# A float32 transformer layer on one core: first feed-forward block in two phases, modulation sums spread over later stages

## The chip, the core and the metric

The kernel runs on one core of a Trainium2 chip. The metric is the device time in microseconds of that core, from start to end of one execution. The median of three runs of the kernel before is 2205.12 us (2204.97 to 2205.4).

## What is computed

One layer over 1024 latent tokens `x` and 256 context tokens `ctx`, width 1024, all in float32: a SwiGLU feed-forward block of hidden width 2816, a mixer (retention heads and chunked gMLP), a second feed-forward block, a last norm. Each of them takes an RMSNorm, shifted and scaled by nine modulation vectors; these come from a product of `silu(c)`, or of `silu(c_ctx)` for context, with a 1024 x 9216 matrix.

```python
m_x = split(silu(c) @ w_ada + b_ada, 9)
m_c = split(silu(c_ctx) @ w_ada + b_ada, 9)
x   = x   + 0.5 * m_x[2] * swiglu(modulate(rmsnorm(x, g0),   m_x[0], m_x[1]), ffn1_w1, ffn1_w2)
ctx = ctx + 0.5 * m_c[2] * swiglu(modulate(rmsnorm(ctx, g0), m_c[0], m_c[1]), ffn1_w1, ffn1_w2)
px = modulate(rmsnorm(x, g1),   m_x[3], m_x[4]) @ w_in     # q, k, v, gate, u, vg
pc = modulate(rmsnorm(ctx, g1), m_c[3], m_c[4]) @ w_in     # its k and v give the first states
...
x = x + m_x[5] * (concat(retention, gmlp) @ w_out)
x = x + 0.5 * m_x[8] * swiglu(modulate(rmsnorm(x, g2), m_x[6], m_x[7]), ffn2_w1, ffn2_w2)
return rmsnorm(x, final_g)
```

The context is read by the mixer's keys and values alone, so it needs modulation rows 0 to 4; rows 5 to 8 serve the latents alone.

## The kernel before

**Float32 products.** Each float32 operand is split into a high part of type fp32r (a copy on ACT, the scalar engine) and a low part (source less high part, on DVE, the vector engine, or POOL). `mm3` (L1593 to L1595) then issues three matmuls: high by high, high by low, low by high. Tokens lie in the free dimension, in `BLOCKS`: context with 256, two latent blocks with 512. Sums stay in 6 of the 8 PSUM banks `PS`.

**Weights.** A unit is 1 MB: 8 blocks of 128 rows by 256 columns. SP's queue loads it to `WR[slot]`, two slots; ACT writes its high part `WH` (L673); POOL its low part `WL` (L520, `unit_low`), in a few places DVE (L1236). The slot is free for the next load when the low part is done (`s_lo`). Each hidden tile of 128 has a unit (gate and up columns) and 128 rows of the down matrix, 0.5 MB, `W2R` to `W2H` (ACT, L734) and `W2L` (POOL, L553).

**Modulation.** 36 modulation units of 1 MB each hold 256 columns of the matrix. The first 12 go through TensorE at the start, as eight short products of `WS` by `CS` (`first_product`, L1639), whose two rows DVE copies out (`first_rows`); `first_columns` turns them to columns, and `first_mods` adds the bias (L1082). The start also norms context and both latent blocks (`norm_sum` on TensorE, `norm_rsqrt` on POOL, `norm_diagonal` L1033 on DVE, `norm_scale` L1613 on TensorE, `norm_apply` and `norm_low`). The next 22 units go through DVE, two in each iteration of the first block: `ada_sums` (L1154), 16 sums a unit for both vectors, in `AS`; `ada_columns` (L1630) lets TensorE add them up over the partitions. The last two lie in the mixer.

**First feed-forward block.** `ffn(FFN[0], ...)` runs `NIT` = 11 iterations on every engine. An iteration has two hidden tiles and three token blocks: 288 matmuls of 512 columns and 144 of 256, in six steps of gate and up, then the down products of the three blocks. ACT makes silu (from gate's bank to `SG`), DVE the product `PR` = `SG` by up's bank, ACT its high part `PH` (L727), DVE its low part `PL` (L1169). The down products are added to `X` and `XC` by DVE.

**Mixer.** 24 units of `w_in` and `w_out`, each read by two to four `FILLS`, which run through a ring of `NRING` = 6 banks in the order of that list. The first are context keys and values (`ck`, `cv`). Latent units have four fills; the last eight units, the "out" ones, have two each, and DVE adds the output to `X`. Their squares for the norm of the second block are made on ACT (`square`), added on DVE (`add_square`).

**Second feed-forward block.** Latents alone. In place of eight quarter products of weights (2 x 2 blocks) and tokens (2 x 2 blocks) a hidden tile takes seven (Strassen's scheme in Winograd's form): DVE makes four sums of weights a tile (`weight_sums`) and, once, four sums of tokens; ACT and POOL split the seven weight blocks; TensorE issues 7 x 12 matmuls and 16 x 3 down products, all of 512 columns; ACT and DVE add the products up through `PU`, `U2`, `U3`. The first tile goes without the scheme (`direct`, 8 x 12 matmuls) while the token sums are made. `block_period` is one tile in the loop.

The order on each engine is the one written in the program, and semaphores alone tie the engines to each other.

## Time and profile before

| | |
|---|---|
| median of three runs | 2205.12 us |
| the profiled execution | 2204.2 us |
| its span | 2202.4 us |
| TensorE's granted clock, mean | 0.989 |
| TensorE busy | 2141.5 us, 97% |
| VectorE (DVE) busy | 1306.7 us, 59% |
| GpSimd (POOL) busy | 659.7 us, 30% |
| ScalarE (ACT) busy | 544.7 us, 25% |
| DMA | 144 MB, mean 66 GB/s |

The span is the time from first to last recorded instruction; the execution's own time is 1.8 us more. A busy TensorE is not TensorE at its peak, since the ends of its matmuls are modelled. By the first column of the timeline the stages are: start to 75.6 us, first block to 1007.9 us, mixer to 1488.0 us, second block to 2179.9 us, and the last norm and the stores. A granted clock of 1.00 is full speed.

### The profile page before, as it was taken

What the parts mean: (1) busy time and instruction counts of PE and PEld (TensorE: products, weight loads), DVE (VectorE), ACT (ScalarE), POOL (GpSimd) and SP (SyncE); (2) the same over time, 40 slices, a digit from 0 to 9 for tenths busy, and PEclk for the clock granted to TensorE, in tenths of its full rate; (3) what the DMA queues carried; (4) which work ended last, traced back from release to release, by engine and by line L of the source; (5) the groups of instructions that cost most, each with busy time, mean ns of one, the idle gap of its engine ahead of it and who ended that gap; (6) DMA issues with size and microseconds to landing.
All of it is one profiled execution on the core that took longest, in us unless ns stands there. A gap on an engine that the chain in (4) does not pass through costs nothing.

```text
span 2202.4 us, 28857 instructions
## 1 busy us (share of the span) xinstructions
PE 2141.5 (97%) x10960; PEld 1798.5 (82%) x10960; DVE 1306.7 (59%) x1997; ACT 544.7 (25%) x819; POOL 659.7 (30%) x340
## 2 busy tenths in 40 slices
PE   8899999999999999998999999998899999999997
PEld 3688888888888888887788899876788888888886
DVE  4754454454454454468725345469677777777767
ACT  3311111111111111124320211335232332222222
POOL 1611111111111121115422213464343443344431
PEclk9999999999999999999999999999999999999998
DMA  9112111111111211113101021220101111101112
GB/s 355 68 48 90 53 48 69 74 48 67 76 48 67 76 48 67 58 58 112 52 16 58 20 87 39 77 100 16 58 31 55 57 57 57 52 33 57 57 39 77
DMA packets 28378, 144.43 MB, mean 66 GB/s; under 512 B 3361, under 2 KB 4641, under 8 KB 15009
## 3 DMA queue, kind: packets, MB, share of 16 engines
q1 hardware_dynamic: 28320, 143.64, 17.6%
q8 instruction: 39, 0.64, 0.1%
q14 instruction: 19, 0.15, 0.0%
HBM read 139.44 MB, written 4.19 MB: 65 GB/s over the span
## 4 chain that ended last, share of the span: by engine, by line
PE 88%; DVE 6%; ACT 1%; issue 1%; POOL 1%; DMA 1%; SPq 0%; DVEq 0%; ACTq 0%; POOLq 0%
PE PS L1593 22%; PE PS L1595 22%; PE PS L1594 22%; PE PS L1846 6%; PE PS L1847 6%; PE PS L1848 6%; PE PS L1639 1%; PE PS L1630 1%; POOL HL L537 1%; PE PS L1788 1%; DVE DG L1033 1%; DMA X<-x 1%; DVE HF L1055 1%; DMA WR<-w_units 1%; DVE ACC L1020 1%
## 5 line engine op out<-in xcount | busy, mean ns | idle before, releaser
L1593 PE MATMUL PS<-HH,WH 128*128 128x512 f32 x1088 | 426.9, 392 | 5.2 <-POOL HL L537 3.3
L1595 PE MATMUL PS<-HH,WL 128*128 128x512 f32 x1088 | 424.1, 390 | 0.0
L1594 PE MATMUL PS<-HL,WH 128*128 128x512 f32 x1088 | 424.0, 390 | 0.0
L520 POOL TENSOR_TENSOR WL<-WR,WH 128x2048 fp32r<-128x2048 f32 x42 | 193.4, 4606 | 535.2 <-ACT WH L673 535.1
L1461 DVE SCALAR_TENSOR_TENSOR X<-PS,GATE,X 128x512 f32<-128x512 f32 x352 | 242.4, 745 | 89.8 <-PE PS L1595 89.7
L1593 PEld LDWEIGHTS PS<-HH,WH 128*128 128x128 f32 x1088 | 204.7, 188 | 48.2 <-issue 4.4
L1595 PEld LDWEIGHTS PS<-HH,WL 128*128 128x128 f32 x1088 | 204.5, 188 | 42.9
L1594 PEld LDWEIGHTS PS<-HL,WH 128*128 128x128 f32 x1088 | 204.8, 188 | 41.9 <-issue 0.7
L1178 DVE TENSOR_TENSOR PR<-SG,PS 128x512 f32<-128x512 f32 (+1 forms) x66 | 39.5, 599 | 296.7 <-ACT SG L725 291.4
L1194 DVE SCALAR_TENSOR_TENSOR X<-PS,GATE,X 128x512 f32<-128x512 f32 x176 | 132.1, 751 | 108.0 <-PE PS L1595 108.0
L725 ACT ACTIVATE SG<-PS 128x512 f32<-128x512 f32 (+1 forms) x66 | 34.5, 523 | 639.6 <-PE PS L1595 639.6
L624 POOL TENSOR_TENSOR WVL<-WR,WVH 128x512 fp32r<-128x512 f32 x84 | 121.1, 1453 | 233.9 <-ACT WVH L747 233.9
L1593 PE MATMUL PS<-PH,W2H 128*128 128x512 f32 (+1 forms) x528 | 188.4, 357 | 0.6 <-DVE X L1194 0.6
L1595 PE MATMUL PS<-PH,W2L 128*128 128x512 f32 (+1 forms) x528 | 187.0, 354 | 0.0
L1594 PE MATMUL PS<-PL,W2H 128*128 128x512 f32 (+1 forms) x528 | 186.8, 354 | 0.0
L553 POOL TENSOR_TENSOR W2L<-W2R,W2H 128x1024 fp32r<-128x1024 f32 x22 | 53.7, 2440 | 374.8 <-ACT W2H L734 374.8
L1154 DVE SCALAR_TENSOR_TENSOR AS<-WR,CS,AS 128x256 f32<-128x256 f32 x336 | 156.4, 540 | 0.0
L1593 PE MATMUL PS<-PXH,W2H 128*128 128x512 f32 x336 | 132.2, 393 | 4.3 <-DVE X L1461 4.3
L1846 PE MATMUL PS<-HH,WVH 128*128 128x512 f32 x336 | 131.9, 393 | 0.0
L1847 PE MATMUL PS<-HL,WVH 128*128 128x512 f32 x336 | 131.9, 393 | 0.0
L1595 PE MATMUL PS<-PXH,W2L 128*128 128x512 f32 x336 | 131.6, 392 | 0.0
L1848 PE MATMUL PS<-HH,WVL 128*128 128x512 f32 x336 | 131.0, 390 | 0.0
(247 smaller groups left out, 4219.8 us busy)
## 6 DMA issues: line engine op xcount, KB each, us to landing
WR<-w_units SPq DMA_DIRECT2D x91, 1024.0 KB, 5.3
W2R<-w_units SPq DMA_DIRECT2D x44, 512.0 KB, 3.6
WS<-ada_units SPq DMA_DIRECT2D x12, 1024.0 KB, 7.7
X<-x SPq DMA_DIRECT2D x2, 2048.0 KB, 14.1
out<-OUT SPq DMA_DIRECT2D x2, 1024.0 KB, 4.2
out<-OUT SPq DMA_DIRECT2D x3, 512.0 KB, 4.1
XC<-ctx SPq DMA_DIRECT2D x1, 1024.0 KB, 5.5
RAW<-w_units SPq DMA_DIRECT2D x1, 1024.0 KB, 6.8
```

What stands on the lines that cost most here:

```text
L520: pool.tensor_tensor(WL[:, slot], WR[:, slot], WH[:, slot].bitcast(F32), ALU.subtract).then_inc(s_lo[slot], 1)
L553: pool.tensor_tensor(w2l[:, j], w2r[:, :], w2h[:, j].bitcast(F32), ALU.subtract).then_inc(s_w2lo, 1)
L624: pool.tensor_tensor(WVL[:, slot], src, WVH[:, slot].bitcast(F32), ALU.subtract).then_inc(s_wl, 1)
L1154: ins = dve.scalar_tensor_tensor(dst, w, c, dst, ALU.mult, ALU.add)
L1194: dve.scalar_tensor_tensor(xv, PS[down_bank(s, k)][:, 0:nt], GATE[:, 0, k, s:s + 1], xv, ALU.mult, ALU.add).then_inc(s_yd, 1)
L1461: dve.scalar_tensor_tensor(xv, y_bank(n)[:, :], GATE[:, 2, d, 0:1], xv, ALU.mult, ALU.add).then_inc(s_fyd, 1)
L1593: pe.matmul(dst, wh, xh, start=first, stop=False)
L1594: pe.matmul(dst, wh, xl, start=False, stop=False)
L1595: return pe.matmul(dst, wl, xh, start=False, stop=last)
L1846: pe.matmul(bank[:, :], wh, xh, start=first, stop=False, skip_group_check=True)
L1847: pe.matmul(bank[:, :], wh, xl, start=False, stop=False, skip_group_check=True)
L1848: ins = pe.matmul(bank[:, :], wl, xh, start=False, stop=k == 3, skip_group_check=True)
```

## The change

1. **First block, phase 1, context alone.** `NF` = 22 steps `p` on each engine: TensorE does gate and up of tile p and the down product of tile p-1, all with 256 columns; down products of all tiles add up in banks 2 to 5 and are added to context once, at the end. POOL takes no part in the loop: the low parts of unit, down weights and `PR` are DVE's. In the steps DVE also makes the modulation sums, by `ada_sums_done`, 24 of them before the loop, 12 a step up to step 12, then 6, and in the steps from 12 on ACT and DVE norm the two latent blocks.
2. **First block, phase 2, latents alone.** The second block's program, now `feed_forward(f)` for both, with a set of semaphores each (`BS[f]`). Units are loaded a second time, down weights too. For f = 0 the first tile is done with `unit_direct` from the last unit of phase 1; the norm of the context (1, 0) lies in its first products, and the scaled context goes out to DRAM (`spill`) and back before the mixer. The last down product's low weights have a buffer of their own, `LASTW`, in both blocks.
3. **Modulation.** `ADA_PE` = 8 units through TensorE at the start, 12 in phase 1, each with both vectors; the 16 others, for the latents alone, in the mixer's units 4 to 19: the modulation unit is loaded to the raw slot `WR` as soon as the unit's low part is done, `latent_sums` makes eight sums in it, `latent_columns` two short matmuls, and only then the slot takes unit i+2.
4. **Start.** Only context is normed there; POOL splits units 0 and 1 of phase 1 there.
5. **Second block.** Low parts of the fourth token sum go from DVE to POOL, and the order of the low parts of tile 1 is `ORDER1`, with one more of them on DVE.

In the diff `NF` is 22 and `FIRST_UNITS` 23.

Constants and the schedule of the sums:

```diff
+FIRST_UNITS = NF + 1
+ADA_PE, ADA_CTX = 8, 20
+ADA_EARLY = 24
+ADA_STEP = 12
...
+MIX_FIRST, MIX_LAST = 4, 19
...
+def ada_sums_done(p):
+    return min(ADA_EARLY + ADA_STEP * (p + 1), 180 + 6 * max(0, p - 12), 16 * (ADA_CTX - ADA_PE)) if p >= 0 else ADA_EARLY
```

SP: phase 1's loads (nine of the steps load a modulation unit behind them, two the latents), and the mixer's:

```diff
+            for p in range(NF):
+                b = p + 3
+                if b < FIRST_UNITS:
+                    sp.wait_ge(s_lo[(b + 1) % 2], (p + 1) // 2 + 1)
+                    unit(first_source(b % NF), (b + 1) % 2)
+                if p + 1 < NF:
+                    sp.wait_ge(s_w2lo, p + 1)
+                    sp.dma_start(W2RB[:, :], w2_units[p + 1]).then_inc(s_w2raw, 16)
+                if p < 6:
...
+            for i in range(2, len(MIX_UNITS)):
+                sp.wait_ge(s_lo[i % 2], unit_count(i - 2))
+                if MIX_FIRST <= i - 2 <= MIX_LAST:
+                    a = ada_after(i - 2)
+                    sp.dma_start(WR[:, i % 2], ada_source(a)).then_inc(s_first[a % 8], 16)
+                    sp.wait_ge(s_col, a + 1)
+                unit(w_units[mix_unit(i)], i % 2)
```

POOL: the start, and what stands ahead of the first period of phase 2:

```diff
+            pool.wait_ge(s_negh, 1)
             norm_rsqrt(0, 0)
+            unit_low(1, 1)
+            unit_low(0, 2)
+            norm_low(0, 0)
...
+                    weight_low(1, 0)
+                    pool.wait_ge(s_yb, NF)
+                    weight_low(1, 1)
+                    weight_low(1, 2)
+                    norm_rsqrt(1, 0)
+                    pool.wait_ge(s_rb, J[1, 0] + 1)
+                    for m in range(3, NM):
+                        weight_low(1, m)
+                    down_low(0)
+                for k in range(4):
+                    token_low(3, k)
```

ACT: phase 1:

```diff
+            def down_high(p):
+                if p:
+                    act.wait_ge(s_yb, p)
+                act.wait_ge(s_w2raw, 16 * p + 16)
+                act.activation(W2HB[:, :], W2RB[:, :], ACT.Copy).then_inc(s_w2hi, 1)
+            for p in range(NF):
+                if p:
+                    down_high(p - 1)
+                if 1 <= p < FIRST_UNITS - 1:
+                    act.wait_ge(s_gu, p)
+                    high(p % 2, 16 * ((p + 1) // 2 + 1))
+                act.wait_ge(s_gu, p + 1)
+                if p:
+                    act.wait_ge(s_prod, p)
+                act.activation(SG[:, :], PS[p % 2][:, 0:CTX], ACT.Silu).then_inc(s_silu, 1)
+                act.wait_ge(s_prod, p + 1)
+                if p >= 2:
+                    act.wait_ge(s_yb, p - 1)
+                act.activation(PH[:, p % 2, :], PR[:, :], ACT.Copy).then_inc(s_ph, 1)
+                if 12 <= p < 16:
+                    b = 1 + (p - 12) // 2
+                    act.wait_ge(s_x[b], 16)
+                    for k in range(4):
+                        square(0, b, p % 2 * 4 + k)
+                if p in (16, 17, 19, 20):
+                    b, k = (1, 4 * (p - 16)) if p < 18 else (2, 4 * (p - 19))
+                    act.wait_ge(s_adv, ADA_CTX - ADA_PE)
+                    for k in range(k, k + 4):
+                        token_modulated(b, k)
+                    norm_high(0, b, k - 3, k + 1)
+            down_high(NF - 1)
```

DVE: phase 1, then the start of phase 2:

```diff
+            for p in range(NF):
+                if p:
+                    down_low(p - 1)
+                if 1 <= p < FIRST_UNITS - 1:
+                    block_low(p + 1)
+                if p and ada_units_done(p - 2) > ada_units_done(p - 3):
+                    dve.wait_ge(s_col, ada_units_done(p - 2))
+                    for a in range(ada_units_done(p - 3), ada_units_done(p - 2)):
+                        ctx_mods(a)
+                for n in range(ada_sums_done(p - 1), ada_sums_done(p)):
+                    ada_sum(n)
+                if p in (13, 14):
+                    for k in range(4):
+                        add_square(0, 1, 4 * (p - 13) + k)
+                if p == 15:
+                    norm_mean(0, 1)
+                    norm_diagonal(0, 1)
+                if p == 16:
+                    gate(0)
+                    gain(1)
+                    dve.wait_ge(s_coef, 3)
+                if p in (15, 16):
+                    for k in range(4):
+                        add_square(0, 2, 4 * (p - 15) + k)
+                if p in (16, 17):
+                    dve.wait_ge(s_rb, J[0, 1] + 1)
+                    for k in range(4):
+                        scaled(0, 1, 4 * (p - 16) + k)
+                if p == 17:
+                    norm_mean(0, 2)
+                    norm_diagonal(0, 2)
+                if p in (17, 18):
+                    tokens_low(1, 4 * (p - 17), 4 * (p - 16))
+                if p in (19, 20):
+                    dve.wait_ge(s_rb, J[0, 2] + 1)
+                    for k in range(4):
+                        scaled(0, 2, 4 * (p - 19) + k)
+                if p in (20, 21):
+                    tokens_low(2, 4 * (p - 20), 4 * (p - 19))
+                dve.wait_ge(s_silu, p + 1)
+                if p:
+                    dve.wait_ge(s_pl, p)
+                dve.tensor_tensor(PR[:, :], SG[:, :], PS[p % 2][:, CTX:2 * CTX], ALU.mult).then_inc(s_prod, 1)
+                ctx_low(p)
+            down_low(NF - 1)
...
+                    dve.wait_ge(s_wraw, 16)
+                    dve.wait_ge(s_lo[1], FIRST_UNITS // 2 + 1)
+                    weight_sums(1)
+                    for k in range(4):
+                        dve.wait_ge(s_hl, 8 * J[0, 1] + k + 1)
+                        dve.wait_ge(s_hf, 8 * J[0, 2] + k + 1)
+                        dve.tensor_tensor(B11[:, k, :], B12[:, k, :], B11[:, k, :], ALU.subtract).then_inc(s_v[0], 1)
+                    for k in range(4):
+                        dve.wait_ge(s_hl, 8 * J[0, 2] + 4 + k + 1)
+                        dve.wait_ge(s_v[0], 4 * f + k + 1)
+                        dve.tensor_tensor(B12[:, k, :], B22[:, k, :], B12[:, k, :], ALU.subtract).then_inc(s_v[2], 1)
+                    for k in range(4):
+                        dve.wait_ge(s_v[2], 4 * f + k + 1)
+                        dve.tensor_tensor(B22[:, k, :], B22[:, k, :], B11[:, k, :], ALU.subtract).then_inc(s_v[1], 1)
+                    dve.wait_ge(s_yb, NF)
+                    for k in range(KT):
+                        xv, c = XCB[:, k, :], k % 2 * CTX
+                        dve.scalar_tensor_tensor(xv, PS[2 + k // 2][:, c:c + CTX], GATE[:, 0, k, 1:2], xv,
+                                                 ALU.mult, ALU.add).then_inc(s_xcd, 1)
+                    for k in range(4):
+                        dve.wait_ge(s_v[1], 4 * f + k + 1)
+                        dve.tensor_tensor(B21[:, k, :], B21[:, k, :], B22[:, k, :], ALU.subtract).then_inc(s_v[3], 1)
+                    add_squares(1, 0)
+                    dve.wait_ge(s_g1, 1)
+                    dve.wait_ge(s_m[1], 1)
+                    dve.tensor_tensor(PU[:, 0, :], SG1[:, :], PS[A0][:, :], ALU.mult).then_inc(s_fp[0], 1)
+                    norm_mean(1, 0)
+                    for k in range(4):
+                        dve.wait_ge(s_v[3], 4 * f + k + 1)
+                        token_low(1, k)
+                    norm_diagonal(1, 0)
+                    for k in range(4):
+                        token_low(0, k)
+                    dve.wait_ge(s_rb, J[1, 0] + 1)
+                    for k in range(KT):
+                        dve.tensor_tensor(XCB[:, k, :], XCB[:, k, :], PS[4][:, 0:CTX], ALU.mult).then_inc(s_xm, 1)
+                    dve.wait_ge(s_g2, 1)
+                    dve.wait_ge(s_m[6], 1)
+                    dve.tensor_tensor(UP2[:, :], G2[:, :], PS[2][:, :], ALU.mult).then_inc(s_fp[1], 1)
+                    gated_low(0, 0, 0)
```

DVE: modulation in the mixer's fills:

```diff
+                if n == FIRST_FILL[i] + (kind(i) == "lat"):
+                    if MIX_FIRST < i <= MIX_LAST + 1:
+                        latent_mods(ada_after(i - 1))
+                    if MIX_FIRST <= i <= MIX_LAST:
+                        latent_sums(i)
```

TensorE: phase 1's loop, the start of phase 2, and the mixer:

```diff
+            def ctx_gate_up(p):
+                slot, bank = (p + 1) % 2, PS[p % 2]
+                pe.wait_ge(s_lo[slot], p // 2 + 1)
+                if p >= 2:
+                    pe.wait_ge(s_prod, p - 1)
+                for half in range(2):
+                    cols = slice(half * P, (half + 1) * P)
...
+            for p in range(NF):
+                ctx_gate_up(p)
+                if p:
+                    ctx_down(p - 1)
+                if p in (14, 16):
+                    pe.wait_ge(s_mods, ada_units_done(p - 2))
+                    norm_sum(0, 1 if p == 14 else 2)
+                if ada_units_done(p - 1) > ada_units_done(p - 2):
+                    pe.wait_ge(s_mods, ada_units_done(p - 2))
+                    pe.wait_ge(s_ms, 1 + (p > 14) + (p > 16))
+                    for a in range(ada_units_done(p - 2), ada_units_done(p - 1)):
...
+                    pe.wait_ge(s_lo[1], FIRST_UNITS // 2 + 1)
+                    pe.wait_ge(s_prod, NF - 1)
+                    pe.wait_ge(s_hl, 8 * (J[0, 1] + 1))
+                    unit_direct(A0, 0, False, 0, 4, s_m[0])
+                    unit_direct(A0, 0, False, 4, KT, s_m[1])
+                    ctx_down(NF - 1)
+                    pe.wait_ge(s_prod, NF)
+                    unit_direct(B_, 0, True, 0, KT, s_m[5])
+                    norm_sum(1, 0)
+                    pe.wait_ge(s_xcd, KT)
+                    pe.wait_ge(s_hl, 8 * (J[0, 2] + 1))
+                    unit_direct(2, 1, False, 0, 4, s_m[2])
+                    unit_direct(3, 1, True, 0, 4, s_m[4])
+                    norm_scale(1, 0)
+                    unit_direct(2, 1, False, 4, KT, s_m[6])
+                    unit_direct(3, 1, True, 4, KT, s_m[3])
+                    product(1, 1, 0)
+                    pe.wait_ge(s_g1, 1)
+                    product(1, 1, 1)
...
+                    if MIX_FIRST < i <= MIX_LAST + 1:
+                        latent_columns(ada_after(i - 1), 1 - slot)
+                    pe.wait_ge(s_lo[slot], unit_count(i))
```

## Rows read from the trace of the kernel before

**Rows 1.** Page, part 4: shares of the chain that ended last, by engine.

```profile
PE 88%; DVE 6%; ACT 1%; issue 1%; POOL 1%; DMA 1%; SPq 0%; DVEq 0%; ACTq 0%; POOLq 0%
```

**Rows 2.** Windows: stretch, length, busy PE, PEld, DVE, ACT, POOL (xcount), PEclk, DMA share, GB/s.

```profile
20.00:30.00 10.00, 8.17 (x40) 3.62 (x39) 6.16 (x12) 4.90 (x8) 0.00 (x0) 1.00 1.02 399
...
246.56:252.21 5.65, 5.65 (x50) 5.65 (x48) 0.75 (x1) 0.00 (x0) 0.00 (x0) 1.00 0.00 0
246.56:330.80 84.24, 84.24 (x450) 72.97 (x449) 40.29 (x69) 13.43 (x17) 14.05 (x4) 1.00 0.17 62
...
1419.30:1430.20 10.90, 10.90 (x50) 9.03 (x49) 3.08 (x5) 3.09 (x4) 4.61 (x1) 1.00 0.28 96
...
1699.90:1730.14 30.24, 30.24 (x134) 24.75 (x133) 22.82 (x28) 9.05 (x15) 12.34 (x8) 1.00 0.14 52
```

**Rows 3.** Timeline, TensorE, first block: start us, length us, engine, line, operation, [idle before].

```profile
27.97 3.62 PE L1639 MATMUL PS<-WS,CS 128*2 128x256 f32 x16
...
75.59 0.39 PE L1593 MATMUL PS<-HCH,WH 128*128 128x256 f32 x1 [2.21 <-DVE MODS L1082]
...
307.16 1.84 PE L1630 MATMUL PS<-ONES,AS 128*128 128x1 f32 x16
```

**Rows 4.** Timeline, ACT, first block.

```profile
253.37 0.42 ACT L727 ACTIVATE PH<-PR 128x256 fp32r<-128x256 f32 x1 [0.58 <-DVE PR L1178]
253.69 1.04 ACT L734 ACTIVATE W2H<-W2R 128x1024 fp32r<-128x1024 f32 x1
...
279.20 1.92 ACT L673 ACTIVATE WH<-WR 128x2048 fp32r<-128x2048 f32 x1 [2.94 <-DMA WR<-w_units]
```

**Rows 5.** Timeline, DVE, first block and the mixer's first unit.

```profile
253.82 0.42 DVE L1169 TENSOR_TENSOR PL<-PR,PH 128x256 fp32r<-128x256 f32 x1 [0.48 <-ACT PH L727]
...
266.55 7.77 DVE L1154 SCALAR_TENSOR_TENSOR AS<-WR,CS,AS 128x256 f32<-128x256 f32 x14
...
282.42 3.67 DVE L1169 TENSOR_TENSOR PL<-PR,PH 128x256 fp32r<-128x256 f32 x1 [0.49 <-ACT PH L727]
...
293.97 5.63 DVE L1154 SCALAR_TENSOR_TENSOR AS<-WR,CS,AS 128x256 f32<-128x256 f32 x14
...
1022.79 2.29 DVE L1236 TENSOR_TENSOR WL<-WR,WH 128x2048 fp32r<-128x2048 f32 x1
```

**Rows 6.** Timeline, POOL, first block, one iteration.

```profile
266.41 2.48 POOL L553 TENSOR_TENSOR W2L<-W2R,W2H 128x1024 fp32r<-128x1024 f32 x1 [9.21 <-ACT W2H L734]
...
281.20 4.61 POOL L520 TENSOR_TENSOR WL<-WR,WH 128x2048 fp32r<-128x2048 f32 x1 [12.31 <-ACT WH L673]
```

**Rows 7.** Timeline, TensorE, end of the first block and the mixer's start.

```profile
1007.50 0.39 PE L1595 MATMUL PS<-PH,W2L 128*128 128x512 f32 x1
...
1010.28 1.17 PE L1613 MATMUL PS<-DG,ONES 128*128 128x512 f32 x2 [2.39 <-DVE DG L1033]
1012.35 0.55 PE L1593 MATMUL PS<-WH,HCH 128*128 128x256 f32 x1 [0.91 <-POOL HCL L537]
...
1013.13 0.41 PE L1593 MATMUL PS<-WH,HCH 128*128 128x256 f32 x1
1013.35 0.41 PE L1594 MATMUL PS<-WL,HCH 128*128 128x256 f32 x1
...
1057.87 0.47 PE L1593 MATMUL PS<-HH,WH 128*128 128x512 f32 x1 [3.32 <-POOL HL L537]
```

**Rows 8.** Timeline, TensorE, second block: start, its one wait, last down product.

```profile
1488.04 0.39 PE L1593 MATMUL PS<-HH,WVH 128*128 128x512 f32 x1
...
1567.68 0.79 PE L1846 MATMUL PS<-V3H,WVH 128*128 128x512 f32 x1 [5.62 <-ACT U L769]
...
2179.64 0.39 PE L1595 MATMUL PS<-WVH,WVL 128*128 128x512 f32 x1
```

**Rows 9.** An "out" unit: POOL's timeline, then DMA issues (KB each, median us to landing).

```profile
1421.11 4.61 POOL L520 TENSOR_TENSOR WL<-WR,WH 128x2048 fp32r<-128x2048 f32 x1 [6.12 <-ACT WH L673]
...
WR<-w_units SPq DMA_DIRECT2D x5, 1024.0 KB, 4.7
```

1769 lines of the change are left out of this document (902 added, 867 removed).

## The prediction, made before any run of the change

> **What bounds the kernel now.** I read the chain that ended last first: 88% of the span lies on TensorE [rows 1]. Then the busy time by stretch: one iteration of the first feed-forward loop is 84.24 us and TensorE is busy in all of it; a period of the second block is 30.24 us and full too; an "out" unit of the mixer is 10.90 us and full [rows 2]. So the order of matmuls is the bound, and what it costs is a count times a pitch. The pitch comes from the same rows: 48 matmuls of 256 columns in 5.65 us are 0.118 us each, 48 of 512 columns in 10.90 us are 0.227 us each [rows 2]. Last I read the few places where TensorE waits [rows 3, 7, 8], since the change rebuilds three of them.
>
> **What is removed.** An iteration before has 288 matmuls of 512 columns and 144 of 256, eleven times. After, context has 22 steps of 72 matmuls of 256 columns (the same 1584), and the latents have 96 + 48 for the first unit and 84 + 48 for each of 21 others: 2916 in place of 3168. 252 x 0.227 = 57.2 us less. Four first products with their columns go too, 4 x 4.1 = 16.4 us (a product is 3.62 us [rows 3]). If nothing else moved, the time would be about 2130 us. I don't forecast that, for five reasons.
>
> **The start.** Before, the stream starts at 75.59 us [rows 3]. After, eight products at 4.1 us, the second from 12.6 us, end at 42 us. But DVE has 24 modulation sums among them, and POOL now splits two weight units there, at about 35.3 (unit 0 is 11 MB behind the start of a queue that moves 399 GB/s [rows 2]) and 41.8 us, 4.6 us each [rows 6]. The trace shows what a POOL operation of this kind does to a DVE one with two SBUF inputs: a 0.42 us subtraction took 3.67 us beside the 4.61 us split, and 14 sums took 7.77 in place of 5.63 us beside one of 2.48 us [rows 5, 6]. So both splits stop the sums: the product of modulation unit 6 is copied at 42.4, that of unit 7 at 50.2 (after the second split, 46.4, and eight sums at 0.40 us), and the last eight sums end at 53.7. Norm, copy and first low part take 2.5 us: the stream starts at 56 us, 19.5 us earlier. Unhindered it would be 48 us, that is the bound on the other side.
> The Trainium skill (SBUF — State Buffer, Who interferes with whom) has this as an exclusive lock, held for the whole instruction, between GpSimd and a DVE instruction with two SBUF inputs. The rows agree.
>
> **Phase 1, context alone.** TensorE needs 72 x 0.118 = 8.5 us a step, 9.3 with the modulation columns (8 of them took 1.84 us [rows 3]; here 4). But nothing of ACT and DVE is spread over latent work any more. The order written out for a step, from the product on DVE to the next: product and ACT's copy 0.46 + 0.42 (the copy starts right behind the product's end), ACT's down weights 1.04 and unit copy 1.92 [rows 4], together to 3.7 us; DVE's low part of the unit 2.29 [rows 5], to 5.9; twelve sums at 5.63/14 = 0.40 us, to 10.8. POOL is idle, so no lock. Twelve steps of 10.8 = 130 us. From step 13 ACT does four squares (2.2 us), or four modulations and four copies (4.3 us), ahead of the weight copies, and DVE adds squares, scales and low parts of tokens, 2.4 us per four. By the same sum the nine steps are 12.9, 12.9, 12.5, 13.3, 17.4, 12.9, 8.5, 15.3 and 12.9 = 119 us. Step 17 is the longest: copies to 8.1, low part to 10.4, scaling to 12.8, mean, power and diagonal to 14.8, token low parts to 17.3. With the first product of the gate at 66 us, the last is at 66 + 130 + 119 = 315 us, and the latents start 2.5 us before it, at 312: 256 us for 22 x 9.3 = 205 us of matmuls.
>
> **Phase 2.** 2916 x 0.227 = 661 us, 2.9 for the last context down product, and 0.3 us a period that a 30.24 us period has over 132 x 0.2267 (6 us). At its start TensorE does 11 us of direct products, then waits at the context's norm sum: ahead of that DVE has four weight sums, sixteen token sums, eight additions to context and eight square sums, from 3 to about 25 us; a wait of 14 us, and about 3 us for the slow clock behind it. Then the second block's own wait comes here too: 5.62 us for U [rows 8], behind a weight load. Together 696 us, which is near the 691.8 us from 1488.04 to 2179.87 that the second block takes with its waits [rows 8]. The first block ends at 312 + 696 = 1008 us, where it ends now (1007.9 [rows 7]): start 19.5 and products 57 us on one side, phase 1 and the transition on the other.
>
> **Into the mixer.** Now 4.5 us go by from the last down product to the first context key, and that one starts at half clock, pitch 0.21 us [rows 7]. After, context is normed long before, and three square sums in place of eight stand ahead of DVE's norm of the latents, which starts 8 us earlier relative to the block's end. The wait of 3.32 us at 1057.87 [rows 7] is the end of that DVE chain, so I take 8 us off (bounds 4 and 12).
>
> **The mixer.** Sixteen columns of two take 0.43 us each, one of eight goes: +5 us. The sums themselves, eight at 0.40, lie beside fills of 5.4 us where a unit has four. An out unit has two. There the raw slot is lent to the modulation unit, so the load of unit i+1 starts only when the columns of i-1 are done, at the start S of unit i. Load 4.7, ACT 1.92, POOL 4.61 [rows 4, 9]: ready at S + 11.8, over 10.9. Worse, ACT waits for that load before it squares, DVE adds the square after it, at S + 7.7, and POOL has the lock from 7.1 to 11.8; then 3.4 us of sums, on which TensorE's columns wait: S + 16. Without lock it is S + 13.2. I take 15 for units 17 to 19, some 3.5 for the first and 0.9 for the last: 3.5 + 3 x 4.1 + 0.9 = +17 us (bounds 5 and 21).
>
> **Second block.** Four token low parts go from DVE to POOL, one low part comes back: DVE is 2 us ahead where TensorE waits. -2 us (bounds -5 and +3).
>
> **The sum.** Against the profiled execution, 2204.2 us: 0 - 8 + 5 + 17 - 2 = +12. The median of the runs, 2205.12, lies 0.9 above that execution: 2217 us.
>
> **Rivals.**
> *The chains hide.* If ACT and DVE run ahead in phase 1, a step costs TensorE's 9.3 us: 12 x 1.5 = 18 us off in the first twelve and up to 119 - 9 x 9.3 = 35 in the others; if the start isn't blocked, 8 more; if the out chain is at its lower bound, 12. Half of the sum of 73 is -36: 2181 us. For it: every duration in my chain is one seen beside other work. Against: the chain has no slack in its order, each link waits for the one before. Chance 0.32, from 2150 to 2200.
> *The clock falls.* In phase 1 TensorE waits 1.5 us in each step and some 4 us in the late ones. The granted clock is 1.00 in all full stretches [rows 2], but after 2.4 and 0.9 us of waits with one short matmul between them the keys ran at half clock (1.2 GHz), 0.21 us a matmul [rows 7], and after the 5.62 us wait of the second block too. At that pitch a step is 72 x 0.213 + 1.7 = 17 us and decides over 10.8. If this holds for half the steps, 11 x 5 = 55 us: 2272 us. It decides as soon as a step's wait takes the clock down for over 6 us; the 2.6 us waits of the trace did not. Chance 0.10, from 2235 to 2290.
> The Trainium skill (TensorE: Matmul & The Clock Gate, HAM oscillation — how this bites in real kernels) warns of just this: groups of matmuls with waits between them that pay the climb each time. No stretch of this trace has such a rhythm.
> *The terms cancel*: the forecast's costs at their lower bounds, within 0.2% of now. 0.17.
> That the change doesn't do what it says I rule out by the counts: the sums, the seven products and the context are all there.
>
> **How the numbers follow.** Forecast 2217 us, 2210 to 2235, chance 0.41. 0.2%, 4.4 us, is about what a measurement of this kernel can tell from no change. Faster 0.32, same 0.17, slower 0.41 + 0.10 = 0.51. For eight in ten the range leaves out 0.1 at the slow end (the clock) and 0.1 at the fast one: 2178 to 2240.
>
> **What would show it.** The stream's start near 56 us; in phase 1 a rhythm of 10.8 us with DVE near 85% busy and TensorE near 80%, a longest step near 17 us; the first latent product near 312; a wait of some 14 us behind the direct products; the end of the first block near 1008; out units of 15 to 16 us in place of 10.9. A rhythm near 9.3 us, or out units of 11 to 12, would make the forecast wrong towards faster; a granted clock under 0.9 in phase 1 towards slower.

## The result, and the profile after

| | before | after |
|---|---|---|
| median of four runs | 2205.26 us | 2268.18 us |
| ratio, 95% interval | | 1.0282 (1.0266 to 1.0299) |
| span of the profiled execution | 2202.4 us | 2266.3 us |
| TensorE's granted clock, mean | 0.989 | 0.965 |

The change makes the kernel 2.8% slower. I had forecast 2217 us, slower by 0.5%, with 2178 to 2240 as the range: the side was right, the size and the range were not. The kernel after, its page (busy time, the 40 slices, the chain of waits):

```profile
span 2266.3 us, 29186 instructions
PE 2114.7 (93%) x10596; PEld 1771.5 (78%) x10596; DVE 1611.2 (71%) x2246; ACT 690.1 (30%) x1083; POOL 758.6 (33%) x454
...
PEclk8999889999999999988999999889999999999998
...
PE 72%; DVE 15%; ACT 6%; issue 4%; DMA 2%; POOL 1%; SPq 0%; DVEq 0%; ACTq 0%; POOLq 0%
```

TensorE's busy time fell by 27 us, though 73.6 us of its work went (the 57.2 and 16.4 us of the prediction): matmuls at half clock (the mean clock is 0.965 for 0.989) and the added columns take up the rest; how it divides between the two was not worked out. Its share of the chain fell from 88% [rows 1] to 72%, and DVE's rose from 6 to 15%.

**Where the time went.** The same event in both traces gives the account by stage; in the mixer that is ACT's high part of a unit. The differences are the profiled executions', and my forecast's differences stand beside them.

| event | before | after | difference | forecast |
|---|---|---|---|---|
| stream starts | 75.59 | 55.81 | -19.8 | -19.5 |
| first latent product of phase 2 | | 311.23 | | 312 |
| high part of unit 2 | 1020.84 | 1034.59 | +13.7 | -8 |
| of unit 6 | 1070.67 | 1097.70 | +27.0 | -8 |
| of unit 17 | 1396.92 | 1433.71 | +36.8 | -3 |
| of unit 23 | 1472.51 | 1534.56 | +62.0 | +14 |
| span | 2202.4 | 2266.3 | +63.9 | +12 |

Phase 1 went as worked out. The timeline of DVE, two steps of it, the product `PR` of the last step, and ACT's weight copies in between (start us, length us, engine, line, operation, [idle before]):

```profile
107.08 0.42 DVE L1372 TENSOR_TENSOR PR<-SG,PS 128x256 f32<-128x256 f32 x1
107.99 0.42 DVE L1312 TENSOR_TENSOR PL<-PR,PH 128x256 fp32r<-128x256 f32 x1 [0.48 <-ACT PH L822]
108.94 1.23 DVE L1316 TENSOR_TENSOR W2LB<-W2RB,W2HB 128x1024 fp32r<-128x1024 f32 x1 [0.53 <-ACT W2HB L807]
110.74 2.29 DVE L1321 TENSOR_TENSOR WL<-WR,WH 128x2048 fp32r<-128x2048 f32 x1 [0.57 <-ACT WH L761]
...
113.02 4.84 DVE L1272 SCALAR_TENSOR_TENSOR AS<-AW,CS,AS 128x256 f32<-128x256 f32 x12
117.77 0.42 DVE L1372 TENSOR_TENSOR PR<-SG,PS 128x256 f32<-128x256 f32 x1
...
311.12 0.42 DVE L1372 TENSOR_TENSOR PR<-SG,PS 128x256 f32<-128x256 f32 x1
```
```profile
107.86 1.05 ACT L807 ACTIVATE W2HB<-W2RB 128x1024 fp32r<-128x1024 f32 x1
108.81 1.90 ACT L761 ACTIVATE WH<-WR 128x2048 fp32r<-128x2048 f32 x1
```

It is the chain of the prediction: product, copy, two weight copies, low part, sums. From step 0 (65.23) to step 11 (180.44) a step is 115.2 / 11 = 10.5 us; the last product comes at 311.12. What the chain leaves of the three gaps on DVE (0.48, 0.53 and 0.57 us) will matter below.

**The end of the first block** is where the account turns. DVE, ACT, POOL and TensorE there:

```profile
993.81 4.04 DVE L1432 SCALAR_TENSOR_TENSOR X<-PS,GATE,X 128x512 f32<-128x512 f32 x6
1001.40 0.80 DVE L1155 COPY ACC<-SQ 128x512 f32<-128x512 f32 x1 [3.54 <-ACT SQ L775]
...
1002.78 5.03 DVE L1158 TENSOR_TENSOR ACC<-ACC,SQ 128x512 f32<-128x512 f32 x1
...
1016.68 3.62 DVE L1155 COPY ACC<-SQ 128x512 f32<-128x512 f32 x1
...
1025.26 3.06 DVE L1158 TENSOR_TENSOR ACC<-ACC,SQ 128x512 f32<-128x512 f32 x4
```
```profile
992.55 4.04 ACT L1024 ACTIVATE XC<-XC,MODS,GAIN 128x256 f32<-128x256 f32 x8
996.49 2.55 ACT L1028 ACTIVATE HCH<-XC 128x256 fp32r<-128x256 f32 x8
998.95 1.89 ACT L761 ACTIVATE WH<-WR 128x2048 fp32r<-128x2048 f32 x1
1000.75 1.13 ACT L775 ACTIVATE SQ<-X 128x512 f32<-128x512 f32 x2
...
1034.59 1.92 ACT L761 ACTIVATE WH<-WR 128x2048 fp32r<-128x2048 f32 x1 [7.13 <-DMA WR<-w_units]
```
```profile
997.04 5.75 POOL L689 TENSOR_TENSOR HCL<-XC,HCH 128x256 fp32r<-128x256 f32 x8 [16.49 <-ACT HCH L1028]
1002.75 4.52 POOL L597 TENSOR_TENSOR WL<-WR,WH 128x2048 fp32r<-128x2048 f32 x1
1015.45 4.56 POOL L597 TENSOR_TENSOR WL<-WR,WH 128x2048 fp32r<-128x2048 f32 x1 [8.19 <-ACT WH L761]
1019.97 1.19 POOL L603 TENSOR_TENSOR RS<-MS,NEGH 128x4 f32<-128x4 f32 x1
```
```profile
1002.91 0.50 PE L1818 MATMUL PS<-WVH 128*128 128x512 f32 x1 [3.88 <-DVE X L1432]
1008.62 0.77 PE L1818 MATMUL PS<-WVH 128*128 128x512 f32 x1 [4.74 <-DVE X L1432]
...
1020.06 0.63 PE L1820 MATMUL PS<-WVH,LASTW 128*128 128x512 f32 x1
```

ACT scales the context, copies it and copies unit 0's weights, 8.2 us, before the first square. DVE adds square k between output additions, so it stands still for 3.54 us and TensorE's last down products with it. Then DVE's second addition takes 5.03 us in place of 0.67, beside POOL's low part of unit 0, and a copy 3.62 us beside that of unit 1; the norm's power `RS` is behind that low part on POOL. Last, unit 2's load is issued behind the rope tables, which wait for the last output addition: it lands 7.8 us after its issue.

The last matmul of the block's down products, the last line of TensorE above, starts at 1020.06, and before at 1007.50 [rows 7]. So 12.6 of the 13.7 us at unit 2's high part stand already there, and the way from that matmul to unit 2 is 14.5 us in place of 13.3.

**The first modulation unit of the mixer.** DVE makes the unit's sums only behind the decay masks and two key rotations, and TensorE waits for the columns:

```profile
1091.85 1.01 PE L1865 MATMUL PS<-ONES,WR 128*128 128x1 f32 x4 [7.50 <-DVE WR L1288]
```

The load of unit 6 waits for these columns, as every load behind a modulation unit does: unit 6's high part starts at 1097.70, 5.9 us behind them.

**The out units.** All of them, then the first and the second of the four that carry a modulation unit, 17.1 us each (windows: stretch, length, busy PE, PEld, DVE, ACT, POOL, PEclk, DMA share, GB/s), then TensorE at the columns in both, DVE in the first, and DVE, ACT and POOL in the others:

```profile
1435.00:1515.00 80.00, 64.98 (x240) 52.19 (x239) 45.96 (x61) 18.77 (x23) 28.52 (x9) 0.81 0.31 116
1442.00:1459.10 17.10, 11.41 (x38) 9.35 (x39) 11.00 (x15) 3.06 (x3) 7.26 (x4) 0.70 0.32 123
1459.10:1476.20 17.10, 14.81 (x54) 11.83 (x53) 8.66 (x14) 3.07 (x3) 4.60 (x2) 0.80 0.33 124
```
```profile
1447.69 1.02 PE L1865 MATMUL PS<-ONES,WR 128*128 128x1 f32 x4 [8.14 <-DVE WR L1288]
...
1464.82 1.02 PE L1865 MATMUL PS<-ONES,WR 128*128 128x1 f32 x4 [2.29 <-DVE WR L1288]
```
```profile
1436.13 4.34 DVE L1285 TENSOR_SCALAR WR<-WR,CS 128x256 f32<-128x256 f32 x1 [1.17 <-DMA WR<-w_units]
1440.50 7.13 DVE L1288 SCALAR_TENSOR_TENSOR WR<-WR,CS 128x256 f32<-128x256 f32 x7
...
1474.21 0.75 DVE L1770 SCALAR_TENSOR_TENSOR X<-PS,GATE,X 128x512 f32<-128x512 f32 x1 [8.19 <-PE PS L1820]
1474.88 3.01 DVE L1158 TENSOR_TENSOR ACC<-ACC,SQ 128x512 f32<-128x512 f32 x1
...
1495.30 3.61 DVE L1288 SCALAR_TENSOR_TENSOR WR<-WR,CS 128x256 f32<-128x256 f32 x7
```
```profile
1470.74 1.91 ACT L761 ACTIVATE WH<-WR 128x2048 fp32r<-128x2048 f32 x1 [12.20 <-DMA WR<-w_units]
```
```profile
1472.73 4.61 POOL L597 TENSOR_TENSOR WL<-WR,WH 128x2048 fp32r<-128x2048 f32 x1 [12.50 <-ACT WH L761]
```

In [rows 2] such a unit was 10.90 us with TensorE full at a clock of 1.00. Here ACT waits 12 us for the load, the square's addition stands beside POOL's low part (3.01 us), the sums and the columns follow, and the mean clock is 0.81 over them. The first of the four isn't like the others: its eight sums take 11.5 us on DVE, beside POOL's unit and token low parts (1435.70 to 1445.79), in place of 4.0 as in the others; TensorE waits 8.14 us for the columns, and its clock is 0.70. In each of the three behind it the wait is 2.3 us and the clock 0.80. Of the 6.2 us that such a unit takes over 10.9, 2.3 are this wait, 0.9 the columns, and the other 3 the half clock: 14 or 15 matmuls behind the columns start 0.43 us apart in place of 0.227.

### The profile page after: what moved, and what is told of

The parts are those of the page before. It is cut to its first block, busy times and chain, and to the rows that moved or that the text cites. A ratio compares the mean times of both kernels' runs of the same rounds, so it can differ in the third digit from the quotient of the medians.

```text
span 2266.3 us, 29186 instructions
## 1 busy us (share of the span) xinstructions
PE 2114.7 (93%) x10596; PEld 1771.5 (78%) x10596; DVE 1611.2 (71%) x2246; ACT 690.1 (30%) x1083; POOL 758.6 (33%) x454
## 4 chain that ended last, share of the span: by engine, by line
PE 72%; DVE 15%; ACT 6%; issue 4%; DMA 2%; POOL 1%; SPq 0%; DVEq 0%; ACTq 0%; POOLq 0%
PE PS L1970 11%; PE PS L1818 11%; PE PS L1971 11%; PE PS L1972 11%; PE PS L1820 11%; PE PS L1819 11%; DVE AS L1272 3%; ACT WH L761 2%; DVE ACC L1158 1%; DMA WR<-w_units 1%; DVE WL L1321 1%; ACT W2HB L807 1%; DVE WR L1288 1%; PE PS L1874 1%; DVE X L1432 1%
## 5 line engine op out<-in xcount | busy, mean ns | idle before, releaser
L1818 PE MATMUL PS<-PXH,W2H 128*128 128x512 f32 x672 | 264.9, 394 | 4.3 <-DVE X L1432 4.3
L1970 PE MATMUL PS<-HH,WVH 128*128 128x512 f32 x672 | 264.6, 394 | 0.0
L1971 PE MATMUL PS<-HL,WVH 128*128 128x512 f32 x672 | 263.8, 393 | 0.0
L1820 PE MATMUL PS<-PXH,W2L 128*128 128x512 f32 x672 | 263.7, 392 | 0.0
L1972 PE MATMUL PS<-HH,WVL 128*128 128x512 f32 x672 | 263.0, 391 | 0.0
L1819 PE MATMUL PS<-PXL,W2H 128*128 128x512 f32 x672 | 262.3, 390 | 0.0
L623 POOL TENSOR_TENSOR WVL<-ST,WVH 128x512 fp32r<-128x512 f32 x125 | 187.4, 1499 | 99.9 <-ACT WVH L841 99.7
L1818 PE MATMUL PS<-HH,WH 128*128 128x512 f32 x416 | 173.1, 416 | 2.4 <-POOL HL L614 2.3
L1819 PE MATMUL PS<-HL,WH 128*128 128x512 f32 x416 | 168.3, 405 | 0.0
L1820 PE MATMUL PS<-HH,WL 128*128 128x512 f32 x416 | 167.7, 403 | 0.0
L1819 PEld LDWEIGHTS PS<-PXL,W2H 128*128 128x128 f32 x672 | 126.8, 189 | 25.4
```

The source lines that it names most:

```text
L623: pool.tensor_tensor(WVL[:, slot], src, WVH[:, slot].bitcast(F32), ALU.subtract).then_inc(s_wl, 1)
L1818: pe.matmul(dst, wh, xh, start=first, stop=False)
L1819: pe.matmul(dst, wh, xl, start=False, stop=False)
L1820: return pe.matmul(dst, wl, xh, start=False, stop=last)
L1970: pe.matmul(bank[:, :], wh, xh, start=first, stop=False, skip_group_check=True)
L1971: pe.matmul(bank[:, :], wh, xl, start=False, stop=False, skip_group_check=True)
```

## The experiments

Each kernel is the changed one with the edit shown. Where there is one execution of a kernel I compare it by its milestones: the stretch from unit 23's high part to the end is the same program in nearly all of them and takes 726.4 to 733.7 us (731.7 in the kernel after, 729.9 in that before), so a difference of under 7 us in such a total says nothing. A single execution also reaches a stage up to 5 us earlier or later than another; the last section says where part of that lies. So I read the gain of an edit from an event just ahead of its stretch to one just behind it.

**Phase 1: POOL in DVE's place.** In phase 1 POOL makes each unit's low part.

```diff
 DVE:
             for p in range(NF):
...
-                if 1 <= p < FIRST_UNITS - 1:
-                    block_low(p + 1)
 POOL:
             norm_low(0, 0)
...
+            for b in range(2, FIRST_UNITS):
+                unit_low((b + 1) % 2, b + 1)
...
```

> One edit to the changed kernel: in phase 1 the low part of each unit is POOL's (which is idle there, 4.6 us) in place of DVE's (2.29 us). Nothing is left out. Theory A (POOL's operation locks DVE's operations with two SBUF inputs, so the modulation sums wait for its whole length): 4.6 in place of 2.29 us in the chain, a step of 12.5 to 13 us in place of 10.4, 21 steps: 40 to 50 us more. Theory B (POOL works beside DVE): DVE's step is 2.3 us shorter and TensorE's 9.3 us bind, 20 to 25 us less.

Measured 2289.2 us, 21 more. A step is (196.29 - 65.18) / 11 = 11.9 us, 1.4 longer, though DVE has 2.3 us less to do. DVE's and POOL's timeline in that kernel:

```profile
104.03 7.57 DVE L1276 SCALAR_TENSOR_TENSOR AS<-AW,CS,AS 128x256 f32<-128x256 f32 x8
...
115.90 9.13 DVE L1276 SCALAR_TENSOR_TENSOR AS<-AW,CS,AS 128x256 f32<-128x256 f32 x12
```
```profile
104.74 4.60 POOL L597 TENSOR_TENSOR WL<-WR,WH 128x2048 fp32r<-128x2048 f32 x1 [7.20 <-ACT WH L765]
116.53 4.66 POOL L597 TENSOR_TENSOR WL<-WR,WH 128x2048 fp32r<-128x2048 f32 x1 [7.19 <-ACT WH L765]
```

Twelve sums take 9.13 in place of 4.84 us: they stand still for nearly the whole of POOL's 4.66. Theory A holds; its size (12.5 to 13 us a step, 40 to 50 in all) was too large, since one or two sums fit in ahead of POOL, beside ACT's copy. By the Trainium skill (SBUF — State Buffer, Who interferes with whom) a DVE instruction with two SBUF inputs contends with a POOL instruction that reads SBUF; the trace agrees.

**Phase 1: DVE's order.** The first edit moves four sums a step into the gaps on DVE, the second also all sums, squares, scalings and token low parts of the last nine steps.

```diff
             for p in range(NF):
+                early = min(4, ada_sums_done(p) - ada_sums_done(p - 1)) if p else 0
+                for n in range(ada_sums_done(p - 1), ada_sums_done(p - 1) + early):
+                    ada_sum(n)
...
                 if p:
                     down_low(p - 1)
```

> One edit to the changed kernel: in each step of phase 1 the first four modulation sums stand ahead of the low part of the down weights, where DVE waits 0.53 + 0.57 us for ACT's two copies. Nothing is left out. Theory A (a step is the chain product, ACT's copy and two weight copies, low part of the unit, sums, with 1.6 us of DVE idle in it): the four sums (1.6 us) fill the gaps, a step goes from 10.4 to TensorE's 9.3 us, the twelve first steps give 13 us, the later ones with sums 2. Theory B (a step is bound by DVE's busy time or by ACT and DVE in turn, with no slack to fill): the rhythm stays at 10.4 us, 0 to 2 us.

> One edit to the changed kernel: in phase 1 DVE's four first sums and, from step 13 on, all sums, square additions, scalings and low parts of tokens stand ahead of the low part of the down weights, in the time in which ACT copies weights. Nothing is left out. Theory A (a step is one chain with gaps on DVE, the extras need not be in it): 9.1 us a step up to 12, 9 to 11 in the last nine in place of 13.2 on the mean, phase 1 ends near 270 to 280 us in place of 311, 30 to 40 us less in all. Theory B (in the late steps DVE's and ACT's sums of work bind): the late steps stay over 12 us, 18 to 22 us less as in the run that moved the sums alone.

Measured 2248.2 and 2220.9 us, 20 and 47 less (18.3 and 45.4 by the last product), the second more than the 30 to 40 of its theory A. The steps up to 11 take (166.66 - 64.39) / 11 = 9.3 us in the first, 9.3 in the second too: that is TensorE's own time, and the first window below shows it full. The last product comes at 292.9 and 265.8 us in place of 311.1. Windows of the kernel with all edits, whose phase 1 is the second's, and of the kernel after:

```profile
65.00:167.00 102.00, 102.00 (x866) 102.00 (x866) 95.23 (x184) 39.14 (x44) 0.00 (x0) 1.00 0.76 291
```
```profile
65.00:180.00 115.00, 107.17 (x895) 105.78 (x895) 97.35 (x184) 38.36 (x45) 0.00 (x0) 1.00 0.70 266
...
190.00:311.00 121.00, 91.51 (x664) 89.16 (x663) 75.31 (x108) 59.18 (x84) 2.02 (x2) 0.87 0.33 109
```

DVE works as much as before (95 of 102 us); only the order is another. In the last steps the extras lay behind the low part, so DVE stood idle for ACT's token work (5.42 us in step 17) and then ACT for DVE's; ahead of it they run side by side, and a step is 98.8 / 10 = 9.9 us in place of 13.1.

**Start of phase 2.** DVE's additions to context ahead of the second and third token sums.

```diff
-                    for k in range(4):
-                        dve.wait_ge(s_hl, 8 * J[0, 2] + 4 + k + 1)
...
                     dve.wait_ge(s_yb, NF)
                     for k in range(KT):
...
+                    for k in range(4):
+                        dve.wait_ge(s_hl, 8 * J[0, 2] + 4 + k + 1)
...
```

> One edit to the changed kernel: at the start of phase 2 DVE's eight additions to context stand ahead of the second and third token sums, 7.2 us earlier. Nothing is left out. Theory A (TensorE's wait of 11.74 us ends with DVE's context additions and their squares): the wait shrinks by 6 to 7 us, the half clock behind it stays, 5 to 8 us less in all. Theory B (behind that wait DVE is late with the token sums' low parts, so what is won is waited for at the first products): 0 to 3 us less.

Measured 2259.7 us, but the milestones give less than that: TensorE's wait is 9.07 in place of 11.74 us, unit 2's high part comes 3.4 us earlier relative to phase 1's last product. The squares' additions still stand behind all token sums. That is between the two theories. The wait still ends with DVE's additions of squares; that moving those would end it sooner was not run.

**End of the first block.** Three runs: ACT's order alone; POOL's two low parts on DVE; then both together. In the third, POOL makes unit 0's low part first, beside the output additions, and DVE that of unit 1, and unit 2's load is issued ahead of the rope tables, which neither of the other two has.

```diff
 SP:
+            sp.wait_ge(s_lo[0], unit_count(0))
+            unit(w_units[mix_unit(2)], 0)
             sp.wait_ge(BS[0].fyd, NYB + 16 * NF)
...
 ACT:
-            for k in range(KT):
-                act.activation(XC[:, k, :], XC[:, k, :], ACT.Identity, scale=GAIN[:, 1, k, 1:2],
-                               bias=MODS[:, 3 * KT + k, 1:2]).then_inc(s_hf, 1)
...
             for k in range(KT):
                 act.wait_ge(BS[0].fyd, NYB + 16 * (NF - 1) + k + 1)
                 square(1, 1, k)
+                act.activation(XC[:, k, :], XC[:, k, :], ACT.Identity, scale=GAIN[:, 1, k, 1:2],
+                               bias=MODS[:, 3 * KT + k, 1:2]).then_inc(s_hf, 1)
...
 POOL:
...
-            low(0)
-            low(1)
             norm_rsqrt(1, 1)
```

> One edit to the changed kernel: on ACT, at the end of the first block, the context's scaling and its high parts (14.. 6.5 us in two groups, with the high part of unit 0 behind them) are no longer ahead of the eight squares of the first latent block but one pair behind each square. Nothing is left out. Theory A (the end of the block is held by this order on ACT: DVE adds square k between two output additions, TensorE's last down products wait for those additions, 3.88 and 4.74 us): the squares start some 6 us earlier, the first mixer unit does too, 4 to 6 us less in all. Theory B (the lock of POOL's long low part on DVE decides, the 5.03 us addition at 1002.78): the squares come earlier but the additions still stand still beside POOL's low parts, under 2 us. Theory C (the slow clock decides): no change beyond 2 us.

> One edit to the changed kernel: the low parts of the mixer's units 0 and 1 go from POOL (4.5 us each, one of them ahead of the power of the norm) to DVE (2.29 us each), behind the squares they delayed. Nothing is left out. Theory A (order on ACT): DVE has 4.6 us more, POOL's lock is gone, between 2 us more and 2 us less. Theory B (POOL's low parts lock DVE's additions, 5.03 us for a 0.68 us one and 3.62 us for a 0.80 us copy, and the power waits 3.3 us behind the second): 4.4 + 2.8 + 3.3 us come back, 4.6 of DVE's time go, so 4 to 8 us less, and no addition of squares over 1.5 us.

> Edits at the end of the first block alone, to the changed kernel: ACT makes unit 0's high part before the squares and the context's scaling between them, POOL makes unit 0's low part first (beside output additions, whose product lies in PSUM) and no other before the norm, DVE makes unit 1's low part behind the squares, and the load of unit 2 is issued ahead of the rope tables. Nothing is left out. Theory A (order on ACT and POOL's lock are two causes in series, each hid the other's gain in the two runs that took one away): the last output addition at 1010 to 1014 in place of 1025 us, unit 2's high part at 1016 to 1020 in place of 1034.6, 14 to 18 us less in all. Theory B (DVE's own 25 us of additions and squares bind): under 8 us less.

Measured 2260.2, 2269.1 and 2255.8 us. Unit 2's high part is at 1030.86 in the first, 3.7 us earlier (1.4 of it since the period before was earlier, too), so 2.3 us less, between theory A's 4 to 6 and theory B's under 2: the first latent block's squares are ready 8 us earlier, and then the second latent block's stand beside 9.2 us of POOL's low parts, and the power behind these. In the second it is at 1034.94, but that run came 5.2 us later to this stretch (unit 0's high part at 1004.19 in place of 998.95), so 4.9 us less, as theory B has it; no addition takes over 0.8 us. In the third it is at 1021.55, 13.0 us earlier (1.5 of it since the period before was earlier), so 11.5 us less, and the last output addition is at 1015.84 in place of 1024.60:

```profile
993.10 4.63 POOL L599 TENSOR_TENSOR WL<-WR,WH 128x2048 fp32r<-128x2048 f32 x1 [14.06 <-ACT WH L762]
```
```profile
992.30 4.04 DVE L1434 SCALAR_TENSOR_TENSOR X<-PS,GATE,X 128x512 f32<-128x512 f32 x6
996.26 1.75 DVE L1157 COPY ACC<-SQ 128x512 f32<-128x512 f32 x1
```

Six output additions, whose product is in PSUM, take 4.04 us beside POOL's low part as they did without; the first copy with both ends in SBUF waits for its end. Did each cause hide the other's gain, as theory A says? Read at the last output addition, counted from the group of six ahead of it: 30.8 us in the kernel after, 28.4 with ACT's order, 25.4 with the low parts moved, 23.5 with both. So the edits alone give 2.4 and 5.4 us and together 7.3: there they add up, and neither hides the other. What the third run has beyond this lies behind that addition: unit 2's high part follows it by 5.7 us in place of 10.0, 10.2 and 10.5 in the kernel after and the two single runs, in which ACT stood 7.1 to 7.6 us for the load. That is the load's new place, 4.3 us, as far as the trace tells; it was not run alone. The 14 to 18 us of theory A were too much: 12.4 in the total, 11.5 by the stretch.

**First modulation unit of the mixer.**

```diff
                 if (name, a) == ("ck", 1):
+                    latent_sums(MIX_FIRST)
                     masks()
```

> One edit to the changed kernel: on DVE the sums of the first modulation unit of the mixer (unit 4) stand ahead of the decay masks, where DVE waits 6.84 us for ACT, in place of behind two key rotations. Nothing is left out. Theory A (TensorE's wait of 7.50 us at the columns of unit 4 comes from the sums' place behind masks and rotations on DVE, and sets everything behind it back): the wait goes, and the half clock behind it, 8 to 12 us less in all. Theory B (the next wait is late next: the load of unit 6 waits for the columns anyway, or the key rotations hold TensorE's banks): 0 to 4 us less.

Measured 2263.1 us. The wait of 7.50 us is gone; unit 6's high part comes 21.3 us behind unit 5's in place of 28.1. But the next three units take back 1.7, 1.5 and 1.7 us, and the way from unit 0 to unit 5 is 0.7 longer: 1.3 us are left from unit 0 to unit 23. Theory A has the wait, theory B the price. Even unit 6 gets 6.7 us of the 13.3 that it lost: its load still waits for the columns (they are at 1087.38, its high part at 1093.09), and the seven sums now take 8.68 us in place of 3.61, since they stand beside POOL's low part of unit 5. What is late behind it was not taken apart.

**The out units.** First without the last four modulation units; then with the low parts on DVE; then also with unit 22's on POOL again and the square ahead of the weight copy (from the third run):

```diff
                     if MIX_FIRST <= i <= MIX_LAST:
                         latent_sums(i)
+                    if 16 <= i < 21:
+                        unit_low(i + 1)
```

> Leaves work out: the last four modulation units (loads, sums and columns in the mixer's out units 16 to 19) are not made; those modulation rows are twice the bias in their place. Theory A (the out units' rhythm of 17.1 us is the loan of the raw slot to the modulation unit): the out units go back to 10.9 us, 24 to 27 us less in all. Theory B (the out units are longer because DVE's squares, the output additions and the slow clock bind them in the new kernel in any case): the rhythm stays over 13 us, under 14 us less.

> One edit to the changed kernel: the low parts of the out units 17 to 22 go from POOL (4.61 us) to DVE (2.29 us), behind that unit's modulation sums. Nothing is left out. Theory A (chain of columns, load 4.9, ACT 1.9, low part, lock, sums): no lock is left, the addition of the square takes 0.7 in place of 3.0 us, sums end 2.3 us earlier, and the unit's low part ends 2 us after them: a rhythm of 14 to 15 us in place of 17.1, 10 to 13 us less in all. Theory B (load and columns alone bind, not the lock): the rhythm stays at 16.5 us or more, under 3 us less.

> Edits to the changed kernel's out units alone: low parts of units 17 to 21 on DVE behind the sums, that of unit 22 stays on POOL (in the run before it stood on DVE behind a norm and cost a wait of 9.59 us), and ACT squares the addition before ahead of the next unit's high part. Nothing is left out. Theory A (lock and the place of the square lengthen the out rhythm): 13 to 14 us in place of 17.1, 11 to 16 us less in all. Theory B (DVE or the load is late next): a rhythm of 15 to 17 us, under 8 us less.

Measured 2236.1, 2267.0 and 2255.1 us. Without the four modulation units the out units are back at 10.9 us, and the window is the one of [rows 2]:

```profile
1473.90:1484.80 10.90, 10.90 (x51) 9.06 (x50) 3.28 (x6) 3.09 (x4) 4.61 (x1) 1.00 0.29 107
```

From unit 17 to unit 23 that is 71.6 us, against 100.9 in the kernel after and 75.6 before: the loan costs 29 us for four units. With the low parts on DVE the rhythm is 14.5 to 13.6 us, as theory A has it, but not its 10 to 13 us in all. Of the gain of 15 us from unit 17 to unit 23 (85.7 for 100.9) 10 were lost again behind unit 23, nearly all in one wait of TensorE, since unit 22's low part now stood behind a norm on DVE; and this execution reached unit 17 3.9 us later:

```profile
1526.02 0.80 PE L1820 MATMUL PS<-HH,WH 128*128 128x512 f32 x1 [9.59 <-DVE WL L1610]
```

The third run has it on POOL: unit 23 at 87.1 us behind unit 17 in place of 100.9, 13.8 us less, and 13.1 in the total. The lock and the place of the square are half of the loan's price of 29 us. The other half, in which load, copy and sums still stand in series (rhythm 13.1 to 16.2 us, mean clock 0.94), was not taken apart.

**All edits together.**

> All edits together: phase 1's order, the start of phase 2, the end of the first block, the first modulation unit of the mixer, the out units. Nothing is left out. Theory A (the causes are separate stretches of the chain and add up): 35 + 6 + 12 + 5 + 13 = 71 us less than the changed kernel, 2190 to 2205 us, which is 0 to 0.7% faster than the kernel before. Theory B (what one stretch gives the next takes back, in the second block or by the clock): 2210 to 2235 us.

Measured 2196.15 us (five runs, 2193.3 to 2200.35); against the kernel before 0.9955 (0.9941 to 0.9969). It is 72 us less than the changed kernel. By milestones phase 1 gives 44.9 of them (45.4 alone), the way to unit 3 10.5 more (3.4 and 11.9 alone), unit 6 8.2 (6.7), of which 3.3 are given back up to unit 17, and the out units 12.1 (13.8); the second block takes 2 back. Only the way to unit 3 falls short, by some 5 us, and not at its ends: this execution took 517.3 us for 17 periods of the first block (one hidden tile of the latents each), 30.43 a period, for which the kernel after took 514.5 and the two single runs 513.9 and 513.7. Without the periods the start of phase 2 gives 1.4 (2.8 alone) and the end of the block 11.9 (10.6 alone). So the stretches add up, as theory A has it. With the change's work unaltered, and only its order and the engine of some low parts mended, it is 0.45% faster than the kernel before.

```profile
span 2195.9 us, 29187 instructions
...
PE 2095.3 (95%) x10596; PEld 1751.4 (80%) x10596; DVE 1602.1 (73%) x2252; ACT 693.4 (32%) x1083; POOL 734.8 (33%) x448
```

## Why the prediction was half right

The side was right, and the start, phase 1 and phase 2 went as worked out. The step that failed is the one into the mixer, a gain of 8 us where the runs show a loss of 13.7; the terms for the mixer's latent units and for the out units were too small.

**The start** held: 55.81 for 56 us, the product of unit 6 copied at 42.09 (forecast 42.4) and that of unit 7 at 49.65 (50.2), both behind sums that waited for POOL's splits.

**Phase 1** held, step by step: 10.5 for 10.8 us; the nine long steps took 13.1, 13.4, 12.6, 13.7, 17.4, 13.2, 8.3, 15.6 and 13.2 us, for 12.9, 12.9, 12.5, 13.3, 17.4, 12.9, 8.5, 15.3 and 12.9. The rival that the chains hide was wrong for the order as written, but it was right that there was room: the second of the two runs got 14.3 of its 18 us up to step 12, down to the 9.3 us of TensorE, and 30.6 of its 35 us in the others, by moving DVE's work and nothing else.

**Start of phase 2** held: a wait of 11.74 for 14 us, 311.23 for 312. The terms given for phase 2 (661, 2.9, 6, 14, 3 and 5.6 us) add up to 692.5, not to the 696 of the sum; the 3.5 us are a slip and decide nothing.

**Into the mixer** failed, and is the largest miss: -8 forecast, +13.7 measured, 21.7 us. The step said that the context is normed long before and three square additions stand ahead of the norm in place of eight. It counted DVE's queue and left out ACT's and POOL's: what the change moved to the end of the block (context scaling, its high and low parts, two unit splits) stands there ahead of the squares on ACT and of the power on POOL. The lock that I had priced for the start I did not look for here. So 12.6 us were lost ahead of the block's last down product, where the forecast had none, and the 8 us behind it didn't come: the norm of the latents did not start earlier. By the runs, ACT's order, POOL's low parts and the late load are 11.5 of the 21.7; the rest, with the half clock behind the waits in it, was not taken apart.

**The mixer's latent units**: +5 forecast, +23.1 measured. I had said that the sums lie beside fills of 5.4 us. For the first unit they lay behind masks and rotations, +13.3 with the slow clock after the wait; moving them gave back 6.7 there, and 1.3 by unit 23. The other eleven took 336.0 in place of 326.2 us; columns of 0.45 us are 5 of these 9.8, the others were not taken apart.

**The out units**: +17 forecast (bounds 5 and 21), +25.2 from unit 17 to unit 23. The mechanism was the one named, loan, lock, sums, columns; the period was 17.1 us in place of 15. Of my two values I took 15 where the sum with the lock said 16; I had not priced the half clock, 3 us in each of three units, by which the output addition that DVE takes first comes at 1474.21, nor the first unit's wait of 8.14 us. From one high part to the next the first unit costs 8.6 us more than before where I had 3.5, the three behind it 6.2, 6.2 and 6.4 for 4.1 each, and the last gives 2.2 back where I had 0.9 more. The run without the loan gives 29.

**Second block**: -2 forecast, +1.9 measured, within what this stretch varies by.

Together 21.7 + 18.1 + 8.2 + 3.9 = 51.9 us, which is 63.9 less the 12 of the forecast.

**The rivals.** The clock's rival had 2272 us, and the time is 2268; that is chance. It wanted half clock in the steps of phase 1, and up to step 12 the clock is 1.00 there. In the late steps it is 0.87, where DVE's chain decides anyway. The half clock comes elsewhere, behind the waits at the block's end and in the out units: TensorE waits 8.14 us in the first of these and 2.3 in each of the other three, at a mean clock of 0.81, and without the modulation units, at 10.9 us and full, the clock is 1.00. That is the rhythm that the Trainium skill (TensorE: Matmul & The Clock Gate, HAM oscillation — how this bites in real kernels) warns of; the trace has it in the mixer, not where I looked for it.

**The range** left out everything over 2240 but the clock. My price for a change that rebuilds three stage boundaries had one of them favourable and unbounded on the bad side: the bounds for the mixer's entry were 4 and 12 us, both gains.

## What to carry to other kernels

Where work is moved to a stage boundary, write out the queue of every engine there, with each operation that the change puts on it, and ask for each addition that the norm waits for what stands ahead of its input; bound such a boundary on both sides of zero. A chain of two engines in turn has gaps on each: independent work goes ahead of the wait, not behind it, which gave 45 us of phase 1 here. And where two edits together give more than their sum, look at more than one event: here the causes added up at the last output addition, and the surplus at the next event came with a third edit, the load, which the single runs did not have.
